# A two-layer fp32 block on one core: layer one's projection in two passes over halves of the input channels, and three smaller edits

## What is computed

```python
def hybrid_layer(x, c, ...):
    mod = jax.nn.silu(c) @ w_ada + b_ada              # (2048) @ (2048 x 6144)
    shift, scale, gate = jnp.split(mod, 3, axis=-1)
    h = rmsnorm(x, pre_g) * (1.0 + scale[:, None]) + shift[:, None]
    proj = h @ w_in                                    # 2048 x 4608
    q, k, v, gate_a, u, gate_p = jnp.split(proj, SPLIT_POINTS, axis=-1)
    y_a = windowed_gqa(q, k, v, rel_table, sink) * jax.nn.silu(gate_a)
    y_p = multiscale_pool(u, w_pool_grp, pool_scale) * jax.nn.silu(gate_p)
    g = jax.nn.sigmoid(h @ w_merge + b_merge)          # 2048 x 4096
    g_a, g_p = jnp.split(g, N_BRANCHES, axis=-1)
    merged = g_a * (y_a @ w_br_attn) + g_p * (y_p @ w_br_pool)
    return x + gate[:, None] * rmsnorm(merged @ w_out, post_g)
```

## Time and profile before

| | us |
|---|---|
| runs, median | 2326.93 (2324.1 to 2327.34) |
| profiled execution | 2325.86, of which the span from first to last instruction 2324.1 |
| PE busy | 2217.0 (95%), mean granted clock 0.973 |
| DVE busy | 1692.8 (73%) |
| ACT busy | 1062.4 (46%) |
| DMA | 583.49 MB, mean 251 GB/s |

### The profile page before, as it was taken

How to read it: one execution, slowest core, us unless ns; L and a number is a source line. 1 busy time by engine, 2 the same in 40 slices (tenths; PEclk the granted TensorE clock), 3 DMA queues, 4 the chain that set the end, 5 groups by cost and what they waited for, 6 DMA issues and landing times.

```text
span 2324.1 us, 27765 instructions
## 1 busy us (share of the span) xinstructions
PE 2217.0 (95%) x11184; PEld 1863.6 (80%) x11184; DVE 1692.8 (73%) x1981; ACT 1062.4 (46%) x1345; POOL 74.7 (3%) x109
## 2 busy tenths in 40 slices
PE   5499999999999999999999999999999999999998
PEld 2388888888878878788878878878888888888886
DVE  6858867787777777767786887568888886774444
ACT  4143345554346654453455633455444443443432
POOL 0000000100000000000011100000000000000000
PEclk8599999999999999999999999999999999999999
DMA  9878778888985756669877888656676665657553
GB/s 381 332 249 299 277 259 312 297 313 309 313 289 198 252 173 227 233 204 329 288 268 242 286 319 277 237 201 216 218 242 229 235 219 175 204 182 253 188 193 127
DMA packets 244932, 583.49 MB, mean 251 GB/s; under 512 B 11994, under 2 KB 14830, under 8 KB 239428
## 3 DMA queue, kind: packets, MB, share of 16 engines
q1 hardware_dynamic: 232560, 535.93, 66.5%
q0 software_dynamic: 11104, 43.37, 5.5%
q10 hardware_dynamic: 1140, 2.43, 0.3%
HBM read 562.78 MB, written 18.90 MB: 250 GB/s over the span
## 4 chain that ended last, share of the span: by engine, by line
PE 79%; DVE 10%; DMA 7%; ACT 2%; issue 1%; ACTq 0%; DVEq 0%
PE gemm L1816 22%; PE gemm L1777 13%; PE gemm L1779 13%; PE gemm L1778 13%; PE gemm L1817 11%; DVE w_lo L1110 3%; DMA mod_stage<-in_w_mod 3%; DMA w_stage<-in_w_ada 2%; DVE mod_acc L1104 2%; DMA mod_stage<-in_w_ada 1%; PE gemm L1820 1%; PE extra L1597 1%; DVE mod_acc_scale L1088 1%; PE gemm L1819 1%; ACT w_hi L779 1%
## 5 line engine op out<-in xcount | busy, mean ns | idle before, releaser
L1110 DVE TENSOR_TENSOR w_lo<-w_stage,w_hi 128x1024 fp32r<-128x1024 f32 x730 | 861.5, 1223 | 432.5 <-ACT w_hi L779 432.1
L779 ACT ACTIVATE w_hi<-w_stage 128x1024 fp32r<-128x1024 f32 x730 | 731.4, 1051 | 831.1 <-PE gemm L1779 403.8
L1816 PE MATMUL gemm<-operand_main,w_hi 128*128 128x512 f32 x2535 | 912.3, 402 | 15.8 <-DVE proj L1501 14.4
L1817 PE MATMUL gemm<-operand_main,w_lo 128*128 128x256 f32 x2535 | 715.1, 282 | 0.0
L1816 PEld LDWEIGHTS gemm<-operand_main,w_hi 128*128 128x128 f32 x2535 | 480.7, 190 | 129.9 <-DVE w_lo L1110 15.3
L1817 PEld LDWEIGHTS gemm<-operand_main,w_lo 128*128 128x128 f32 x2535 | 483.1, 191 | 7.5
L1777 PE MATMUL gemm<-w_hi,operand_main 128*128 128x512 f32 x960 | 381.6, 398 | 7.3 <-DVE operand_main L1262 5.8
L1778 PE MATMUL gemm<-w_lo,operand_main 128*128 128x512 f32 x960 | 376.4, 392 | 0.0
L1779 PE MATMUL gemm<-w_hi,operand_main 128*128 128x512 f32 x960 | 376.1, 392 | 0.0
L1104 DVE SCALAR_TENSOR_TENSOR mod_acc<-mod_stage,c_silu,mod_acc 128x1024 f32<-128x1024 f32 x180 | 229.0, 1299 | 58.6 <-DMA mod_stage<-in_w_mod 43.0
L1777 PEld LDWEIGHTS gemm<-w_hi,operand_main 128*128 128x128 f32 x960 | 181.8, 189 | 46.9 <-issue 9.8
(11 more groups left out here) (231 smaller groups left out, 1744.5 us busy)
## 6 DMA issues: line engine op xcount, KB each, us to landing
w_stage<-in_w_in SPq DMA_DIRECT2D x129, 1024.0 KB, 6.2
mod_stage<-in_w_mod SPq DMA_DIRECT2D x192, 512.0 KB, 6.1
w_stage<-in_w_up SPq DMA_DIRECT2D x88, 1024.0 KB, 5.0
w_stage<-in_w_down SPq DMA_DIRECT2D x44, 1024.0 KB, 5.0
w_stage<-in_w_merge SPq DMA_DIRECT2D x32, 1024.0 KB, 6.1
w_stage<-in_w_out SPq DMA_DIRECT2D x32, 1024.0 KB, 7.8
w_stage<-in_w_ada SPq DMA_DIRECT2D x31, 1024.0 KB, 7.6
mod_stage<-in_w_ada SPq DMA_DIRECT2D x32, 512.0 KB, 6.0
```

What stands on the lines that cost most here:

```text
L779: return nc.scalar.activation(o, i_, f, **kw)
L1110: tt(WL[:, slot_of(n), c0:c1], WST[:, slot_of(n), c0:c1], WH[:, n % HIS, c0:c1].bitcast(F32), ALU.subtract)\
L1816: mm(G[:, m, :], hi, x_of(k), start=(k == 0), stop=False)
L1817: ins = mm(G[:, m, T:2 * T], lo, x_of(k)[:, 0:T], start=False, stop=False)
```

## The change

1. **Two passes.** The shift and scale of the first 8 tiles of channels (half of the columns of both parts, 16 rows of 1 MB instead of 32) are made first; nine groups `half` of two slabs then run over the first 8 channel tiles, and their sums are put aside in SBUF. During the first eight groups the other half of the 32 rows is loaded and added (`load_second_half`, `second_half`: two half rows at every slab, four buffers). Then PE sums them (`ada_sums`) and nine groups of two slabs `rest` run over the other 8 tiles; DVE adds both PSUM halves to what was put aside.
2. **Rows of parts 2 to 4 move back**: 11 of the 16 rows of part 2 from the projection into `merge`; parts 3 and 4 follow, three rows in a phase where there were two.
3. **Start.** The eight position lines use two buffers, two of them are made earlier, and PE runs four products ahead of the column sums. The store of the lines moves behind the loads of the pooling weights.
4. **Layer-two attention** leaves out the empty quarter: 384 score columns of 512, three transposes of four, one half-width product.
5. **Boundaries**: the turns of row blocks 1 to 3 go inside the slabs before their use.
6. **Last rows**: the root and the additions of the final result are done by halves of the tokens.

```diff
-        one = lambda c: Group(w_in, c, 4, "main", "proj", tile=c // P)
+        half = lambda c: Group(w_in, c, 2, "main", "part", tile=c // P)
+        rest = lambda c: Group(w_in, c, 2, "main", "rest", chunk0=KT // 2, tile=c // P)
+        for n, c in enumerate(first_cols):
+            phases.append(Phase("half", n, [half(c)], ada=2 * n if n < 8 else None,
+                                hooks={0: [("ada_end", 0)], 1: [("ada_end", 1), ("tiles", 2)]} if n == 8 else {}))
-            phases.append(Phase("in", n + 1, [one(c)], mod=(2, 3 * n, 3), slots=(0, 2, 1), hooks=pool(n)))
+            phases.append(Phase("in", n + 1, [rest(c)], hooks={0: ([("pool_out", n - 1)] if n else []) + [("pool_sum", n)], 1: [("pool_mix", n)]}))
...
-                                mod=(3, 2 * i, 2), slots=(0, 2),
-                                post=[("mod_end", 3)] if i == 7 else []))
+                                mod=(2, 5 + 3 * i, 3) if i < 3 else ((2, 14, 2), (3, 0, 3), (3, 3, 3), (3, 6, 3), (3, 9, 4))[i - 3],
+                                slots=(0, 1, 2, 3) if i != 4 else (1, 2, 3), post=[("mod_end", 2)] if i == 3 else []))
...
-                                hooks=behind, mod=(4, 2 * i, 2), slots=(0, 2)))
+                                hooks=behind, mod=(4, 3 * i - 3, 3) if i else (3, 13, 3), slots=(0, 1, 2),
+                                post=[] if i else [("mod_end", 3)]))
...
+            def load_second_half(r):
+                if r == 0:
+                    sp.wait_ge(x_sq, 2)
+                for part in range(2):
+                    j = 2 * r + part
+                    positive(sp, ada_rows, j - 3)
+                    sp.dma_start(AST[j % 4], A["w_ada"][0].rearrange("(c q) n -> c q n", q=P)[r, :, part * D + D // 2:(part + 1) * D])\
+                        .then_inc(ada_landed[j % 4], 16)
...
+                    if ph.ada is not None and ph.ada + s + 2 < KT:
+                        load_second_half(ph.ada + s + 2)
...
+            def second_half(r):
+                for part in range(2):
+                    j = 2 * r + part
+                    dve.wait_ge(ada_landed[j % 4], 16 * (j // 4 + 1))
+                    positive(dve, ada_rows, j - 1)
+                    acc = MACC1[:, part * (D // 2):(part + 1) * (D // 2)]
...
-            first_rows(0, 25)
+            first_rows(0, 13)
             norm_rs(0)
-            stage_mod_end(0)
-            first_rows(25, 28)
+            first_rows(13, 15)
             split_lo(0)
-            first_rows(28, MOD0_ROWS)
+            first_rows(15, MOD0_ROWS)
...
+                    if k == 2 and r == 3:
+                        nc.vector.tensor_reduce(V_OO[:, h:h + 1], S_OO[:, h, :], AX.X, ALU.add).then_inc(sums_made, 1)
+                        if h:
+                            for c in (2, 3):
+                                add_rows(2, c, 0).then_inc(out_row, 1)
+                        root_of(4 + h, V_OO, R1V[:, h:h + 1])
+                        for c in range(4 if h else 2):
+                            add_rows(2, c, h).then_inc(out_row, 1)
...
+                    if g.evac == "rest":
+                        o = PROJ[:, g.kw["tile"] + 2 * u:g.kw["tile"] + 2 * u + 2, :]
+                        wait_evac(dve, part_of[g.col], u + 1)
+                        wait_full(dve, g, u)
+                        link(tt(o, half_of(g, u, 1), o, ALU.add))
                         tt(o, high, o, ALU.add).then_inc(pair_done, 1)
...
                     if ph.ada is not None:
+                        second_half(ph.ada + s)
                     for r in mods_behind(ph, s):
                         mod_row(ph, r)
...
                 if what == "prep_h" and k:
                     keep_busy(ph.groups[0], 8)
                     turn_rows(k - 1, 0)
-                    turn_rows(k - 1, 1)
                     keep_busy(ph.groups[0], 8)
...
+                    if by_tile and ph.name in ("kv2", "up") and q < 3 and (kc, m) == (1, 0):
+                        turn_rows(int(ph.name == "up"), q + 1)
...
-                                q, k = PROJ[64 * a:64 * a + 64, arg["pair"], b * P:(b + 1) * P], KD[64 * a:64 * a + 64, arg["kv"], :]
-                            ins = mm(X[a][:, b * T:(b + 1) * T], q, k, start=True, stop=True)
+                                q, k = PROJ[64 * a:64 * a + 64, arg["pair"], b * P:(b + 1) * P], KD[64 * a:64 * a + 64, arg["kv"], 0:P + b * P]
+                            ins = mm(X[a][:, keys_of(arg, b)], q, k, start=True, stop=True)
...
+            pe.wait_ge(mod0_rows, LAST_ROW - 1)
+            pe.wait_ge(line_copied, HEADS1)
+            for n in range(4):
+                mm(X[0][:, :], IDENT[:, :], LINEB[:, n, :], start=True, stop=True)
+            pe.wait_ge(half_row, 1)
+            ada_sums(MACC, 0, 1, half_summed)
+            pe.wait_ge(mod0_rows, MOD0_ROWS)
+            ada_sums(MACC, 0, 0, half_summed)
```

More of the change, by code:

```diff
@@ L348, in build @@
                     n_dve += g.pairs
-                if g.evac == "row" or not g.in_rows:
+                if g.evac == "row" or not g.in_rows and g.evac != "rest":
                     n_low += g.pairs
@@ L353, in build @@
                 slabs.append((ph, g, q))
-        by_tile_phases = [ph for ph in phases if ph.name in ("in", "kv2", "up") and ph.i == 0]
+        by_tile_phases = [ph for ph in phases if ph.name in ("half", "kv2", "up") and ph.i == 0]
         named = lambda name: [ph for ph in phases if ph.name == name]
         first = lambda name: named(name)[0]
-        MOD0_ROWS = 32
+        MOD0_ROWS = 16
         mod_w = [(A["w_ada"][0], p) for p in range(3)] + [(A["w_mod_2"][0], p) for p in range(6)]
@@ L393, in build @@
         op_ready = sem("operand_ready")
+        ada_landed, ada_rows = [sem(f"ada_landed{n}") for n in range(4)], sem("ada_rows")
         def wait_evac(eng, g, pairs=None):
@@ L576, in load_mod_row @@
                 w, sub = mod_w[part]
+                if part == 2 and row0 + r == 0:
+                    sp.wait_ge(ada_rows, 32)
                 for half in range(2):
@@ L619, in _ @@
                 .then_inc(start["pool_in"], 16)
+            pool.wait_ge(line_copied, HEADS1)
+            pool.dma_start(lines[:, 0:P * LINE].rearrange("h (q k) -> q h k", q=P), LINEB[:, :, :]).then_inc(start["lines_stored"], 16)
             def stage(what, k):
@@ L794, in _, with make_lines @@
             activate(AFF[:, 0:2 * KT], COL[:, 0:2 * KT], ACT.Sigmoid).then_inc(c_ready, 1)
+            def make_lines(h0, h1):
+                act.wait_ge(start["line_in"], 32)
+                for h in range(h0, h1 + 1):
+                    if h < h1:
+                        positive(act, line_mm, h - 1)
+                        activate(TABB[:, h % 2, :], TABX[:, h:h + 1].broadcast_to([33, P]), ACT.Copy).then_inc(line_col, 1)
+                    if h > h0:
+                        act.wait_ge(line_mm, h)
+                        activate(LINEB[:, h - 1, :], X[(h - 1) % 2][:, :], ACT.Copy).then_inc(line_copied, 1)
+            make_lines(0, 2)
             act.wait_ge(const_set, 2)
@@ L1076, in first_rows @@
                 for t in range(r0, r1):
-                    acc = (MACC, MACC1)[t // 16]
-                    for c0, c1 in ((0, D),) if t < LAST_ROW else ((0, D // 2), (D // 2, D)):
-                        if t == LAST_ROW and c0 == 0:
+                    for part in ((0, 2),) if t < LAST_ROW else ((1, 2), (0, 1)):
+                        c0, c1 = part[0] * (D // 2), part[1] * (D // 2)
+                        if t == LAST_ROW and c0:
                             dve.wait_ge(half_row_in, 16)
@@ L1248, in hook @@
                     affine_of(2)
+                if name == "ada_end" and arg == 1:
+                    scale_half(1)
+                    half_sums(1, 0)
+                if name == "tiles":
+                    if arg == 2:
+                        scale_tile(8)
+                        scale_tile(9)
+                    for t in range(4 * arg, 4 * arg + 4):
+                        if t + 2 < KT:
+                            scale_tile(t + 2)
+                        low_tile(t)
                 if name == "poolmix":
@@ L1447, in hook @@
                             .then_inc(gs["y"], 1)
-            ups = [g for g in groups if g.evac == "ffn"]
+            part_of = {g.col: g for g in groups if g.evac == "part"}
             def gain_rows(g):
@@ L1598, in mod_end, with ada_sums @@
                 ins.then_inc(mod_summed, 1)
+            def ada_sums(acc, half, part, signal):
+                for t in range(8):
+                    ins = mm(X[3 - part][:, 8 * half + t:8 * half + t + 1], acc[:, part * (D // 2) + t * P:part * (D // 2) + (t + 1) * P],
+                             ONES[:, 0:1], start=True, stop=True)
+                ins.then_inc(signal, 1)
             def keep_busy(g, n):
```

267 lines of the change are left out of this document (146 added, 121 removed).

## The result

The changed kernel takes 2344.04 us (median of 6 runs, 2337.8 to 2347.63), the kernel before in the same job 2325.51: a ratio of 1.0067, with a 95% interval of 1.0049 to 1.0085. It is slower, where I had forecast 2303. The profiled execution took 2345.39, its span 2343.5, which is 19.4 more than before.

A forecast was written before the change was run, and what follows sets the result against it. Bound by PE with a dead start. Terms -38.4 + 14.9 + 11.5 - 7 - 3 - 1.5 = -23.5 on the profiled 2325.86 give 2302.4, median said 2303; own range 2294 to 2311, with rivals 2285 to 2318.

The forecast's parts named there:

- The loads: First passes: 2.1 MB in 5.65 to 6.4 us, 330 to 370 GB/s, like branch1's 354; no cost taken.
- my terms: First passes: slabs of 5.65 us, 13.6 for waits at group ends, 5.2 for the second half's sums.
- DVE's order: First passes: split, row pair, evacuation in a group's last slab cost 1.2 us in seven groups, 3.6 in the first.
- Rival B: First passes: clock falls at every group end, 8 falls of 1.6 us, 13 more, 2316 us; chance 0.14.
- Rows moved back: Merge, branch1 and out1: DVE falls behind on the additional rows, costing 11.5 us, bounds 0 to 26.
- Second boundary: Turning row blocks inside the slabs saves 1 us here.
- attention: Layer two: leaving out a quarter of three kinds of PE work saves 6.0 us, shorter DVE work 1: -7.
- the first boundary: Block 1's turn with its wait leaves the front of the first product and returns in a slab: -2 us.
- the end: Final additions: two done beside PE's last products, two during the root's wait; -1.5 us, between 0 and -3.
- The start: First product comes at 68.5 us instead of 106.94, a gain of 38.4 us (35.5 to 40.5).
- C: First passes: clock stays low between waits, slabs cost 5.65 us more; +45, 2348 us if eight slabs; chance 0.06.

The follow-up runs named there:

- both edits: Changed kernel with the second half's loads on GpSimd's queue and the evacuation ahead of the row pair: 2314.89 us, ratio 0.9936 to the kernel before.
- the start version: The same kernel as both edits, from which further edits were tried: 2314.89 us, ratio 0.9936 to the kernel before.
- the version with four rows: On top of both edits, rows of parts 2 to 4 placed anew, two a phase in branch1 and 23 in merge: 2308.71 us, ratio 0.9915.
- the third buffer: Three half-row buffers instead of two from merge to out1: 2292.54 us (0.9847) on top of both edits, 2327.16 us (1.0001) on the changed kernel alone.
- the edit alone: Kernel before with only the smaller layer-two attention: 2321.99 us, ratio 0.9979; the four phases took 205.5 us for 210.7.
- the version with the queue alone: Changed kernel with only the second half's loads moved from SyncE's queue to GpSimd's: 2325.69 us, ratio 0.9995 to the kernel before.

## Why the prediction was wrong

**The step that failed** is the sentence "The loads (...) are about what branch1 moves, 354, with PE waiting for nothing; I take nothing for them." I compared bytes. The bytes are carried (321 GB/s with both edits); what the loads cost is their place in SP's queue. The order that I had printed myself shows a slab load behind each pair of row loads, and with two rows' worth of buffers the row load has to wait until DVE has used a row, which is the last thing DVE does in a slab. A load that should run three slabs ahead was so tied to DVE's present work. Price: 21.0 us, falls of the clock included. With the queue free the nine groups take 122.1, where my terms give 120.5 (eighteen slabs of 5.65, 13.6 and 5.2). The other 2.9 of the 25.5 lie in the groups `rest`, where I had nothing for the store beside the row in `u1`, which cost 5.1 in the start version.

The Trainium skill ("Trainium Kernel Development and Optimization", section "Key Constraints") says that DMAs issued from several engines share the same 16 DMA engines, and that this "only saves the sequencer's issue time". By it the move to GpSimd's queue would have given, as an estimate, what SP's issue has on the path, 0.33 us in each of some nine turns of the loop above, 3 us. It gave 21.0: the landing of a slab stayed what it was (median 8.4 us, and 8.5 with the rows on the other queue), only it was asked for earlier. The measurement decides.

**DVE's order** was right in mechanism and size: predicted 1.2 us a group, measured 1.05 to 1.08, and 3.68 at the first group for my 3.6. It was seen only once the queue was gone.

**Rival B**, that the clock falls at each group's end, is half true. Behind the waits of 3.40 to 4.57 us the next slab takes 7.20 to 7.25 for 5.72; behind those of 1.05 to 1.76 it does not. What I lacked was the length of the waits. The passage that I had cited from the Trainium skill ("TensorE: Matmul & The Clock Gate", section "HAM oscillation — how this bites in real kernels") tells of waits of about 3 to 5 us; the trace agrees for those of 3.40 us and more, and the waits of 1.2 us that I had forecast were shorter than the page's.

**Rows moved back:** that DVE falls behind was right (one buffer a half row, a step of 6.4 and 7.2 where I had 7.4, against a slab of 5.44); the size was 24.8 for 11.5. The step that failed is what this does to PE: "what it can lag before PE waits is some 7 us (a split ends 3.7 into slab s and is needed at s+2)". I let DVE lag until `w_lo` is late, from the second or third phase on. PE never waited for `w_lo` there, and the third phase of `branch1` takes 21.76 us, as before. It waited for things of DVE's that are needed at once: operand tiles (3.52 and 4.74 us, where before it had no wait) and the accumulator, which PE's column sum reads directly. The sum waits 3.83, then runs at the lower clock, 6.99 for 3.63, and behind it the second phase starts with a slab of 8.37, where the slab behind this sum took 7.15 before: 8.4 of the 13.3 missing. The rest are the waits for operand tiles and the slower clock behind them. The wait comes back wherever the last row is close to the sum, as the version with four rows shows. Until the third buffer was tried, a limit of the transfers (R3) would have explained the same numbers.

**Second boundary:** I priced the turns of one group, and the change makes them in two: its condition says nothing of the group, which the diff shows. Up0 grew by 4.5 us (three repeated turns of 0.78, a third one within the first group, 0.5 for its operand tile, 0.9 at the fifth slab), and only 1.9 came back ahead of the first product.

**Right:** attention (with the 1 us that the edit alone doesn't show), the first boundary (57.1 us; 57.0 to 58.6 in the other versions that have it), the end (four additions behind the last root, 2.74 us, for eight in 5.39):

```profile
2338.27 2.74 DVE L1241 SCALAR_TENSOR_TENSOR residual_rows<-gained_rows,small,residual_rows 128x512 f32<-128x512 f32 x4
```

The start came at 68.25 for my 68.5, but that is partly luck: I had taken a value between 66.5 at the full clock and 71.4 at the lower, and the late start of the filling products was made up for by their being shorter.

The first loss alone took the whole gain of 23.5 us, the second decided the sign. I had given the loads neither a price nor a range, and none of the rivals was about a queue; with 0.06 for slower I answered only for the clock. That C's 2348 is near the 2344 is chance: the clock came back within the next slab behind each long wait.

## What to carry to other kernels

When an edit adds loads, look not only at the bytes but at what each load waits for, and at what stands behind it in the same queue: a prefetch behind a load whose buffer is freed late is no prefetch. Then follow the loop until it closes and compare its length with the slabs that it yields. An instruction that reads an accumulator directly, such as a sum on the busiest engine, needs distance from the last addition; and where one limit hides another, an edit that does nothing alone may be worth 12 us after the first is removed.

## What the runs showed of the hardware

- Loads started by GpSimd in front of a busy stream cost little: from 75 to 180 us, 28 half rows of 512 KB from its queue landed in 5.9 to 6.7 us (median), where from SP's it was 5.0 to 6.1, and the slabs beside them in 8.5 for 8.4.
- Waits of PE of 1.05 to 1.76 us between slabs at 2.4 GHz were not followed by a fall of the clock in the first passes of the changed kernel and of the version with the queue alone; those of 3.40 us and more were. Between 1.9 and 3.0 us both happen: in eleven versions PE waits 2.2 us in up0's fifth slab, and behind it the clock fell in two of them and stayed in nine.
- Identical stretches differ by several us from execution to execution: from the first og phase to the end of gates2, where all the two-pass kernels run the same instructions, the traces show 298.4 to 305.8 us. Most of that is the clock: its mean is 0.994 in the shortest and 0.972 in the longest, which is 6.8 of the 7.4 us between them. A single pair of profiles can't show a gain of 3 us there.
